# A feed-forward part with half of its norm inside, its last product opened early, and PE's operands placed elsewhere in SBUF

## The reference

```python
h = rms_norm(x, norm2_g[l]) * (1 + sc2) + sh2
u = causal_depthwise_conv(h @ w_up[l], conv_w[l], conv_b[l])
u_gate, u_val = jnp.split(u, 2, axis=-1)
x = x + g2 * ((jax.nn.silu(u_gate) * u_val) @ w_down[l])
```

## The kernel before, in words

| product | moving | stationary |
|---|---|---|
| first projection, tokens on partitions | `p_cut` 172864 (0) | `m1h_hs` 195552 (32) |
| first projection, other jobs | `m1h_hs` 195552 (32) | `p_cut` 172864 (0) |
| merge of the first block | `merge_acut` 170432 (0), to 219584 | `merge_wcut` 145856 (0) |
| `m22o` | `m22o_wcut` 150368 (32) | `m22o_acut` 166752 (32) |
| up product | `m2x_hs` 196576 (32), to 229344 | `m2x_cut` 59264 (0) |
| down product `o3` | `o_wcut` 146048 (0) | `o_acut` 162432 (0) |

## Time and profile before

### The profile page before, as it was taken

One profiled execution on the slowest core, in us unless ns is written; L12 is line 12 of the kernel. 1 busy time (PEld: TensorE's weight loads), 2 busy tenths in 40 slices (PEclk: granted clock), 3 DMA queues, 4 the chain that ended last, 5 costly groups with the idle time before them and its releaser, 6 DMA issues. The chain is left out here.

```text
span 2642.7 us, 25498 instructions
## 1 busy us (share of the span) xinstructions
PE 2163.7 (82%) x7994; PEld 1330.3 (50%) x7994; DVE 1658.0 (63%) x3431; ACT 1016.5 (38%) x2513; POOL 715.6 (27%) x617
## 2 busy tenths in 40 slices
PE   5999978897788687877868887657777777999898
PEld 5778755676332232322324453223333655788787
DVE  5674266535698988878457776747767546455434
ACT  4213346323344343333334344426533535333322
POOL 1020022001344454444434553435443100000000
PEclk7999988998899999898989999789888878999999
DMA  6764200221699999999999999999998532222132
GB/s 207 234 198 116 66 13 25 61 76 74 267 421 421 421 395 421 401 422 407 418 372 420 420 420 418 411 383 373 421 420 360 148 106 71 96 95 95 48 96 96
DMA packets 143115, 682.66 MB, mean 258 GB/s; under 512 B 20064, under 2 KB 36736, under 8 KB 74512
## 3 DMA queue, kind: packets, MB, share of 16 engines
q0 software_dynamic: 73728, 536.90, 49.2%
q1 hardware_dynamic: 69264, 144.27, 16.8%
HBM read 678.99 MB, written 2.10 MB: 258 GB/s over the span
## 5 line engine op out<-in xcount | busy, mean ns | idle before, releaser
L2207 PE MATMUL peer_Y<-peer_w,peer_diag 128*128 128x512 f32 x1792 | 901.6, 642 | 244.3 <-ACT peer_diag L2193 218.0
L2152 POOL DMA_INDIRECT peer_w<-in_peer_uv,peer_eidx x512 | 608.1, 1188 | 747.7 <-PE peer_Y L2207 459.0
L2161 DVE CUSTOM_DVE_ANT_0 peer_w<-peer_w,peer_xtok 128x1024 f32<-128x1024 f32 x512 | 619.6, 1221 | 205.1 <-DMA peer_w<-in_peer_uv,peer_eidx 201.7
L2207 PEld LDWEIGHTS peer_Y<-peer_w,peer_diag 128*128 128x128 f32 x1792 | 337.4, 202 | 756.9 <-ACT peer_diag L2193 452.4
L2185 ACT ACTIVATE peer_gel<-peer_dots 128x1 f32<-128x1 f32 x512 | 103.7, 202 | 717.9 <-DVE peer_dots L2161 717.6
L2193 ACT ACTIVATE peer_diag<-all_ident,peer_a 128x128 f32<-128x128 f32 x448 | 179.9, 402 | 17.5 <-PE peer_Y L2207 2.5
L2187 ACT ACTIVATE peer_a<-peer_gel,peer_gates 128x1 f32<-128x1 f32 x512 | 150.8, 294 | 17.1
L2698 PE MATMUL ffn_acc<-m2x_hs,m2x_cut 128*128 128x512 f32 x352 | 139.1, 395 | 5.6 <-PEq L123 5.6
L2700 PE MATMUL ffn_acc<-m2x_hs,m2x_cut 128*128 128x512 f32 x352 | 141.1, 401 | 0.0
L2699 PE MATMUL ffn_acc<-m2x_hs,m2x_cut 128*128 128x512 f32 x352 | 139.5, 396 | 0.0
L1061 ACT ACTIVATE p_cut<-m1h_raw 128x512 fp32r<-128x512 f32 (+2 forms) x96 | 58.1, 607 | 205.9 <-PE p_acc L1008 120.0
(11 more groups left out here) (493 smaller groups left out, 3620.8 us busy)
## 6 DMA issues: line engine op xcount, KB each, us to landing
m_gates<-in_w_ada SPq DMA_DIRECT2D x48, 512.0 KB, 4.3
m2x_raw<-in_w_up SPq DMA_DIRECT2D x22, 1024.0 KB, 4.8
m1h_raw<-in_w_in SPq DMA_DIRECT2D x80, 256.0 KB, 3.0
m20h_raw<-in_w_in SPq DMA_DIRECT2D x48, 256.0 KB, 7.1
m22h_raw<-in_w_in SPq DMA_DIRECT2D x48, 256.0 KB, 2.8
m_down_ring<-in_w_down SPq DMA_DIRECT2D x22, 512.0 KB, 3.5
peer_w<-in_peer_uv,peer_eidx POOLq DMA_INDIRECT x512
m_out_ring<-in_w_out SPq DMA_DIRECT2D x16, 512.0 KB, 3.5
```

What stands on the lines that cost most here:

```text
L2152: pool.indirect_dma_start(self.w[:, n % self.RW].rearrange("p c n -> p (c n)"), None, self.uv_dram, bass.IndirectOffsetOnAxis(self.col(sel ...
L2161: dve.tensor_tensor_reduce(u, u, self.xtok[:, n // PICKS, :], 1.0, 0.0, ALU.mult, ALU.add, self.col(self.dots, n)).then_inc(self.dotted, 1)
L2207: ins = pe.matmul(self.Y[:, h, :], self.diag[:, i % self.RD, :], self.w[:, n % self.RW, 1, h * BANK:(h + 1) * BANK], start=(k == 0), stop= ...
```

## The change

- **Norm of tiles 2 and 3 inside `ffn_up`.** Phase n4 is gone. Gain and shift factors made for tiles 0 and 1 are kept and used again. ACT and DVE do what they did in n4, all subtractions now on DVE; POOL has the two roots. PE begins with the products of chunk 0 for columns 0 to 255 (48 products of 256 columns), then the 16 transposes, then chunk 1 for columns 0 to 255 (48), and, after the norm of both tiles is in, chunks 0 and 1 for columns 256 to 511 (96). The loop follows as before.
- **Last product opened in `ffn_up`.** Up product and transposes use banks 0 to 3 and 4 to 7 of one PSUM tensor. After its loop PE makes the down product's chunks 0 and 1 for outputs 4 to 7 (24 products, banks 4 to 7). ACT and DVE split these two chunks before they treat the last two up chunks; SP loads chunks 2 and 3. The new phase `out_closing` starts with outputs 0 to 3 of chunks 0 and 1; the rest is as in `out_project`.
- **Places.** `m1h_hs` and `m2x_hs` go to the low side, the rings `m1h_raw`, `m20h_raw`, `m22h_raw` to the high side. `u` and `sl` of `ffn_up` lie in memory kept for attention. Start bytes in the built program (remainder by 64, by 128): `m1h_hs` 156096 (0, 64), `p_cut` 190272 (0, 64), `m2x_hs` 59264 (0, 0), `m2x_cut` 92096 (0, 64), down product's `m_wcut` 178880 (0, 64) and `m_acut` 195264 (0, 64), `m1h_raw`, `m22h_raw` and `m2x_raw` 212960 (32), `m20h_raw` 217056 (32), `m20p_cut` 198912 (from 211200). All of `m22...` moves up by 32832 bytes. The experts' tensors stay.

Cut to its core, the diff:

```diff
+class Opening:
+    R = 2
+    def scalar(self, act, early_landed, made):
+        act.wait_ge(early_landed, 16 * len(self.ring.loads))
+        for c in range(self.R):
+            act.wait_ge(made, c + 1)
+            act.activation(self.acut[:, c, 0, :], self.actT[:, c, :], ACT.Copy)
+            act.activation(self.wcut[:, c, 0, :], self.raw[:, c, :], ACT.Copy).then_inc(self.hi_made, 1)
+    def vector(self, dve):
...
+    def tensor(self, pe):
+        for c in range(self.R):
+            pe.wait_ge(self.lo_made, c + 1)
+            for o in range(NT, 2 * NT):
+                self.product(pe, o, c, False)
+def out_closing(nc, name, o, kchunks, resid, gate, out_dram):
...
+            for c in range(R, kchunks):
+                act.wait_ge(o.landed[c % R], 16 * (c // R))
+                act.wait_ge(used, c - R + 1)
...
+            for c in range(kchunks - R):
+                pe.wait_ge(o.lo_made, c + 1)
+                for b in range(NT if c < R else NO):
+                    ins = o.product(pe, b, c, False)
+                ins.then_inc(used, 1)
...
-        self.hs = ph.sb("hs", [P, 2, KD, SEQ], F32R, side="right")
+        self.hs = ph.sb("hs", [P, 2, KD, SEQ], F32R)
...
-                hs = ph3.sb("hs", [P, 2, KD, KEYS], F32R, side="right")
+                hs = ph3.sb("hs", [P, 2, KD, KEYS], F32R)
-                ring = Early(ph3.sb("raw", [P, KD, BANK]), project_loads(
+                ring = Early(ph3.sb("raw", [P, KD, BANK], side="right"), project_loads(
...
 def ffn_up(...)
-            chunk(0, 0)
+            products(0, slice(0, AFTER))
+            for i in range(n):
+                turn(i)
             pe.wait_ge(lo_made, 1)
-            chunk(1, 0)
+            products(1, slice(0, AFTER))
+            pe.wait_ge(rest_lo, n)
+            for r in range(R):
+                products(r, slice(AFTER, SEQ)).then_inc(done, 1)
             with pe.Fori(1, steps) as i:
...
+            opening.tensor(pe)
...
-        norm_transpose(nc, "n4", consts, resid, ahead.hs, d["norm2_g"], mod=(part(4), part(3)), tokens=later, first_col=later[0] * P)
-        out_project(nc, "o3", gT, d["w_down"], NF, resid, out_ring, gate=kept.rows[:, 1, :], out_dram=out)
+        out_closing(nc, "o3", opening, NF, resid, kept.rows[:, 1, :], out)
```

More of the change, by code:

```diff
@@ L2661, in ffn_loads, with ffn_up @@
     return lambda raw: [(raw[:, r], w_dram[r]) for r in range(2)]
-def ffn_up(nc, hs, cut, w_dram, cw, cb, gT, ring, early):
+def ffn_up(nc, consts, resid, ahead, later, kept, w_dram, cw, cb, gT, ring, opening, early):
     R = 2
@@ L2669, in ffn_up @@
         raw = ring.raw
-        u = ph.sb("u", [P, R, 2, SEQ])
-        sl = ph.sb("sl", [P, R, SEQ])
-        acc = ph.ps("acc", [P, 2 * R, BANK])
+        hs, cut, fac, shift = ahead.hs, ahead.cut, ahead.fac, ahead.shift
+        n = len(later)
+        AFTER = later[0] * P
+        u = kept.av[:].rearrange("p (r g) q -> p r g q", g=2)
+        sl = kept.kT[:, 0:R, :]
+        acc, tp = opening.acc[:, 0:2 * R, :], opening.acc[:, 2 * R:, :]
+        junk = tp.rearrange("p b n -> p (b n)")[:, D:2 * D]
+        xn = gT[:, NF - 2 * n:, :].rearrange("p (i c) q -> p i (c q)", i=n)
+        whole = xn.rearrange("p i (k q) -> p i k q", q=P)
+        ssq, ms, rstd = (ph.sb(x, [P, n]) for x in ("ssq", "ms", "rstd"))
         landed = [ph.sem(f"landed{r}") for r in range(R)]
@@ L2730, in chunk @@
                 act.activation(sl[:, r, :], u[:, r, 0, :], ACT.Silu).then_inc(silued, 1)
+            for i in range(n):
+                if i >= 1:
+                    act.wait_ge(sums, i)
+                act.activation(junk, resid[:, later[i], :], ACT.Square, accum_out=ssq[:, i:i + 1]).then_inc(sums, 1)
             split(1, 0, first=True)
+            for i in range(n):
+                act.wait_ge(turned, 2 * i + 1)
+                for k in range(4):
+                    ins = act.activation(whole[:, i, k, :], tp[:, 2 * i, k * P:(k + 1) * P], ACT.Identity, bias=shift[:, k:k + 1], scale=fac[:, k:k + 1])
+                ins.then_inc(act_out, 1)
+                act.wait_ge(act_out, i + 1)
+                act.wait_ge(dve_out, i + 1)
+                act.activation(hs[:, 0, :, new(i)], whole[:, i], ACT.Copy).then_inc(rest_hi, 1)
             for r in range(R):
@@ L2739, in _ @@
                     chunk(r, i)
+            opening.scalar(act, early_landed, out)
             for r in range(R):
@@ L2826, in second_front, with second_ffn @@
                         side=side(45, 2 * KD - 2) if ahead is None else ahead)
-def second_ffn(nc, consts, resid, mod, d, kept, out, ahead):
-    part = lambda i: mod[:, i * KD:(i + 1) * KD]
+def second_ffn(nc, consts, resid, d, kept, out, ahead):
     with Phase(nc, "m2") as ph:
```

137 lines of the change are left out of this document (117 added, 20 removed).

## The result

| | before | after |
|---|---|---|
| median, five runs of each in turn | 2647.24 us (2641.63 to 2649.72) | 2628.37 us (2624.6 to 2631.72) |
| ratio, 95% interval | | 0.9936 (0.9923 to 0.9948) |
| profiled execution, span | 2644.48, 2642.7 us | 2631.52, 2629.8 us |

Faster by 0.64%, some 17 us, and not by 31.6: 2628.37 lies above the range's end of 2625. The profiled execution of after is a long one of its five, so the two spans differ by only 12.9 us. The forecast of 2611 also stood on the median of three runs of before, 2642.86; five gave 2647.24, so 4.4 of the 17.4 us between 2611 and 2628.37 are the starting value's and 13 the gain's.

A forecast was written before the change was run, and what follows sets the result against it. It took PE to be the bound: the pace of one product in full stretches, idle time and a lower clock at phase changes. Gains 7.9 + 6.4 + 6.4 + 10.9 = 31.6 us from the median 2642.86 gave 2611, range 2606 to 2625.

The forecast's parts named there:

- Part 1: Norm phase and opening of the up product: the loop's first product starts at 2270.8 instead of 2278.63, 7.9 us gained.
- Part 4: Opening of the last product: 24 products fill the idle handover and the clock stays up, 10.9 us gained.
- Part 2: Pace of the up product's loop: 960 products go from 0.2333 to 0.2267 us with both starts at remainder 0, 6.4 us.
- Rival (b): Alignment by 128 counts: the loop gains nothing, the first projection half, 22.0 us in all, 2621; chance 15%.
- Part 3: First projection: 960 products of 512 columns get the same shorter pace, 6.4 us, or 3.2 if 128 counts.
- Priced at nothing: Items given no cost: one more semaphore clearing on POOL, the experts' tensors not moving, the closing's tail staying DVE's.
- Rival (d): Beside the experts, moved ring m20h_raw and m20p_cut: slower writes at the high end could bring 2675; chance 3%.
- Rival (a): Operand places in SBUF do nothing, so only norm and opening gains are left: 18.8 us, 2624; chance 13%.

The follow-up runs named there:

- e2: The changed kernel with its four placements taken back to the sides of before, norm inside and opening kept: 2628.39 us, ratio 0.9929.
- e3: The changed kernel with 192 unused bytes ahead of the feed-forward cut weights, both loop operands starting at 128 modulo 256: 2622.42 us, ratio 0.9901.
- e5: e3 with the first projection aligned too, all operands of its 512-column products starting at 192 modulo 256: 2616.07 us, ratio 0.9898.
- e6: e3 with first-projection norm rows of 2080 bytes, so its operands' offset takes all eight multiples of 32 modulo 256: 2627.2 us in one execution.
- e8: The changed kernel with the last product's opening moved out of the feed-forward part to the head of the closing: 2640.06 us, ratio 0.9975.
- e4: The kernel before with 96 unused bytes ahead of the feed-forward cut weights, both loop operands starting at 224 modulo 256: 2641.49 us, ratio 0.9972.
- e10: The kernel before with only the raw ring beside the experts moved to the right side, starting at 224 modulo 256: 2650.25 us, ratio 1.0013.
- e13: The changed kernel with 224 unused bytes at the top of SBUF, so right-side rings start at multiples of 256: 2625.6 us, ratio 0.9918.
- e1: The kernel before with the change's placements of norm outputs and raw rings alone, no norm inside, no opening: 2647.77 us, ratio 1.0005.

## Why the prediction was wrong

It was wrong by size: right in sign and mechanism for two of four parts, wrong for the other two, and a cost was priced at nothing.

- **Part 1, right in the mechanism, lucky in the size.** 8.3 us for 7.9. The waits were those named, 1.4 us for the subtraction and 1.6 for the taps (1.3 and 1.4 predicted). The lower clock was over by 2251 (PEclk 0.57 before that, 1.00 after it); PE's first four products still had the full one. In e2, e3, e5, e6 and e8 it was over 2 us later, and the gain there is 6.2 to 7.3 us.
- **Part 4, right.** 10.4 us for 10.9 (its terms, 9.8 - 0.9 - 0.8 + 2.7, make 10.8); idle over the phase's end 0.75 (0.9), chunk 2 late by 0.9 (0.8), PEclk 1.00 throughout. e8 gives it back.
- **Part 2, the step that failed.** "With both starts at remainder 0 by 64 I take 0.2267": 6.4 us expected, none came. The pair of remainders was read right in the table of places; the grain was wrong. The cases that made the rule (merge, `m22o`, `o3`) were equal by 64 and equal by 256 at once, so they could not tell. Rival (b) had the mechanism, with 128 in place of 256, its loop gained nothing as here, and it had 15%; its 2621 was 7 us too low. What the runs showed in place of 64 is an offset of 0 modulo 256: after had 0 and 0 by 64 and kept 0.2333, e3 and e4 went at 0.2266 and got the 6.4 us with 192 and 96 unused bytes.
- **Part 3, mis-sized by the same step.** 960 x 6.67 ns = 6.4 us. Over the 576 products the pace fell from 134.60 / 575 = 0.2341 to 0.2316: 1.4 us in the 576 products and by the same 2.5 ns about 1.0 in the other 384, so 2.4. Where all starts are equal (e5) the 576 gain 3.9.
- **Priced at nothing, and not nothing: "the experts' tensors don't move".** The ring beside them does. Rival (d) named ring and stage, with 3% and as a catastrophe of 32 us; its form was right and its size 2.4 us, at most 3.9 by e10. The argument against it (`m2x_raw` lay high before, without a wait in the loop) was about place, and start decides. Nor could the loop have shown it: `m2x_raw` starts at 224 in before and after and at 0 in e13, and the loop takes 223.8 or 223.9 us in all three, its queues at a share of 0.26 or 0.27.
- **Rival (a)** had the gain, 18.8 us (measured 16.9 by the ratio, 18.9 by the medians), for the wrong reason: places count, by some 25 us in this kernel (loop 6.4, first projection 3.9, experts' rows 12, ring 2.4), only the new ones brought little of it. It leaned on the Trainium skill, page "SBUF — State Buffer", section "Who interferes with whom", that PE has two independent read ports and never waits on anyone. In e3 nobody else moved, and the starts of PE's own two operands changed a product of 512 columns by 6.7 ns; where the two differ, the measurement decides.

Summed as measured, 8.3 + 10.4 + 2.4 - 2.4 = 18.7 us, and 16.6 to 17.7 with the longer lower clock of part 1, against 16.9 by the ratio (13.8 to 20.4) and 18.8 by e2. The 3.5 us lost ahead of 104 us are no part of it: e1, with the same placements, didn't lose them, and e4, which is the kernel before in all of that stretch, lost 5.5 us there in its profile, with the clock's lower level at the same place.

Not settled: why a product of 512 columns with unequal starts takes just 6.7 ns more, why one of 256 columns doesn't, why the lower clock at the norm lasts one of two times, what delays the early stretch in some executions, and the 1 to 2 us between the ring's 2.4 us and the stretch's 4.

## What to carry to other kernels

Put both operands of a long row of 512-column matmuls at the same start modulo 256, each row of them (a row length that is no multiple of 256 undoes it; at 256 columns the equal starts were the slower ones here, so measure), and let every tile that a full DMA queue fills start at a multiple of 256. Both cost a few unused bytes, and the list of addresses shows them before anything runs. And where a rule about places is read off a few rows, ask which finer grain those rows can't tell apart, and give that its full chance.
